# A gated delta net in stacked 32-row blocks, in a one-core decoder layer

## The chip, the cores and the metric

The kernel runs on one core of a Trainium2 chip. TensorE (PE) multiplies matrices, VectorE (DVE), ScalarE (ACT) and GpSimd (POOL) do the rest, and SyncE (SP) issues DMAs. The metric is the device time of one execution in microseconds: a median of 1965.41 over three runs (1960.49 to 1966.39).

## The reference, cut to what matters

One layer of a decoder for 1024 prompt tokens and 8 samples of 8 tokens: a norm, one input projection, three mixers (sparse attention, a gated delta net, S5), an output projection and an MLP. The delta net has 4 heads of 64. Queries and keys pass a short convolution and silu, then:

```python
q = l2norm(y[..., :DN_WIDTH].reshape(B, L, DN_HEADS, DN_DK)) * DN_DK ** -0.5
k = l2norm(y[..., DN_WIDTH:2 * DN_WIDTH].reshape(B, L, DN_HEADS, DN_DK))
# in chunks; gc is the running sum of the log decay, tri the lower triangle
decay = jnp.where(tri, jnp.exp(jnp.where(tri, diff, 0.0)), 0.0)     # diff = gc_i - gc_j
a_mat = jnp.where(strict, jnp.einsum('nbhid,nbhjd->nbhij', kb, kc) * decay, 0.0)
sol = lax.linalg.triangular_solve(a_mat + eye, rhs, left_side=True, lower=True)
u, w = sol[..., :dv], sol[..., dv:]
a_qk = jnp.where(tri, jnp.einsum('nbhid,nbhjd->nbhij', qc, kc) * decay, 0.0)
# chunk after chunk:
v_new = u_i - w_i @ S ;  o_i = (q_i * exp(g_i)) @ S + aqk_i @ v_new
S = S * exp(g_last) + (k_i * exp(g_last - g_i)).T @ v_new
```

## The kernel before, in words

Stages follow one another, each a block of five instruction streams with a barrier at its end: input norm with feature projection and S5, query projection, token projection, delta net, key preparation, attention of the samples, attention of the prompt, output projection and MLP. Arithmetic is f32; projections split f32 into two rounded parts and take three products.

The query projection (`query_projection`, L544, by `project`, L404) has 12 units (4 column chunks, 3 token groups). Beside its products DVE convolves six feature rows (L580) and ACT applies silu (L590). ACT and DVE copy the units out by turns.

The delta net (`delta_net`, L1093) takes chunks of 128 tokens, two by two in pairs: (0,1), (2,3), (4,5), (6,7), and the 64 sample rows alone. For a chunk PE turns features into rows (`rows_of`, L1500); ACT squares and copies them (`squares_of`, L1288), DVE sums squares per head and POOL takes the power -1/2 (L1237); DVE scales (`normalise`, L1377); POOL multiplies by gates (`scale`, L1233); PE turns everything back (`turn`, L1510), ACT copies (`features_of`, L1299). PE makes decay rows, with a second product adding a -1e30 table above the triangle (L1536, L1538), ACT their exponential (`decay_of`, L1310), PE the Gram products (`grams`, L1521), and DVE multiplies (`decayed`, L1394).

The inverse of the triangular matrix is built in seven levels over whole 128x128 matrices. In each, POOL masks A to the level's blocks, PE multiplies by T ("lower", L1565), ACT copies the result to U, PE joins (L1575, L1576), DVE subtracts from T and its transpose TT:

```python
pool.tensor_tensor(B[:n, x, :, :n], AT[:n, k % 4, :, :n], mask, ALU.mult).then_inc(b_ready, 1)
last = pe.matmul(m.ps[:n, 3 * x, h * P:h * P + n], B[:n, x, h, :n],
                 T[:n, x, h, :n] if s else m.ident[:n, :n], start=True, stop=True)
```

After a pair's levels comes its chain, chunk by chunk: w (L1584), v (L1626, L1629), state and output (L1633 to L1641), the state by DVE (L1434). The order is written out by hand: `after_level` puts the preparation of the next pair's chunks behind certain levels; the chain stands alone behind them. At the end DVE masks the sample rows' operands (L1468 to L1471), norms the outputs (`finish`, L1443) and PE turns them (L1651).

Of the kernel before, what the change touches and what calls it, by code (L numbers as in the profile page):

```python
# [22 lines left out]
P = 128  # L23
# [9 lines left out]
SEQ = 1024  # L33
# [33 lines left out]
def constant_tables():  # L67
# [42 lines left out]
    t["neg"] = np.where(p <= i, 0, NEG).astype(f)  # L110
    t["neg_s"] = np.where((p <= i) & (p // 8 == i // 8), 0, NEG).astype(f)
    t["level"] = np.concatenate([((i >> s) == (p >> s) + 1) & (i >> (s + 1) == p >> (s + 1))
                                 for s in range(LEVELS)], 1).astype(f)
    t["seq_col"] = np.concatenate([np.broadcast_to((np.arange(64)[None, :] // 8) == b, (P, 64))
                                   for b in range(8)], 1).astype(f)
    t["seq_row"] = np.concatenate([(p // 8) == b for b in range(8)], 1).astype(f)
    t["quarter"] = (p // 32 == np.arange(4)[None, :]).astype(f)
# [393 lines left out]
def token_projection(nc, m, tokens):  # L511
# [25 lines left out]
    def gpsimd(pool, _):  # L537
        pool.memset(m.small[64:128, TS, :], 0.0).then_inc(zeroed, 1)

# [4 lines left out]
def query_projection(nc, m):  # L544

    with ExitStack() as ctx:
        units = [(c, n) for c in range(4) for n in range(3)]
        convw = ctx.enter_context(nc.sbuf_tensor("convw", [P, 6, 4], F32))
        conv = m.mixT[:, 0:6, :]
        loaded, tap, conv_made, silu_made = (m.sem(f"conv_{n}") for n in ("loaded", "tap", "made", "silu"))  # L550
# [14 lines left out]
        def load(pool, _):  # L565
            pool.dma_start(convw[:], m.conv_w).then_inc(loaded, 16)

# [4 lines left out]

        def vector(dve, u):

            if u % 3 == 2 or u // 3 * 2 >= 6:
                return
            f = u // 3 * 2 + u % 3
            if f == 0:
                dve.wait_ge(loaded, 16)
            for j in range(4):  # L580
                src, w = m.dnx[:, f, j:j + CONVN], convw[:, f, j:j + 1]
                if j == 0:
                    dve.tensor_scalar(conv[:, f, :CONVN], src, w, None, ALU.mult).then_inc(tap, 1)
                else:
                    last = dve.scalar_tensor_tensor(conv[:, f, :CONVN], src, w, conv[:, f, :CONVN], ALU.mult, ALU.add)
                    last.then_inc(conv_made if j == 3 else tap, 1)
                if j < 3:
                    dve.wait_ge(tap, 3 * f + j + 1)
# [8 lines left out]
        def scalar(act, u):  # L597
            if u % 3 == 2 and u // 3 * 2 < 6:
                silu(act, u // 3 * 2)
                silu(act, u // 3 * 2 + 1)  # L600

        project(nc, m, "qp", m.w_in[:4], [P] * 4, units, evacuation, True,
                side={"gpsimd": load, "sync": load_next, "vector": vector, "scalar": scalar}, preload=m.query_raw)
# [489 lines left out]
def delta_net(nc, m):  # L1093
# [6 lines left out]
    with ExitStack() as ctx:  # L1100
# [3 lines left out]
        NT = TILES  # L1104
        flat_hT = m.mixT[:].rearrange("p k n -> p (k n)")
        conv, convs = m.mixT[:, 0:6, :], m.convs
        names = ["ones", "ones_s", "upto", "upto_s", "neg", "neg_s", "level", "seq_row"]
        C = {n: sb(n, [P, CONST_AT[n][1]]) for n in names}
        alog, dtb, normw = sb("alog", [P, H]), sb("dtb", [P, H]), sb("normw", [P, HD])
        minus_half = sb("minus_half", [P, NT * H])  # L1110
# [5 lines left out]
        qk = sb("qk", [P, 2, 512])  # L1116
        sq = sb("sq", [P, 512])
        ssq = sb("ssq", [P, 2, 8])
        rnorm = sb("rnorm", [P, 2, 8])

        kb, kbg, qg = sb("kb", [P, 256]), sb("kbg", [P, 4, 256]), sb("qg", [P, 256])
        kdec, vb = sb("kdec", [P, 4, 256]), sb("vb", [P, 4, 256])
        featT = sb("featT", [P, 6, P])
        qgT = sb("qgT", [P, 4, 2, P])
        decay = sb("decay", [P, H, P])
        AT, aqkT = sb("AT", [P, 4, H, P]), sb("aqkT", [P, 4, H, P])
        B, U, T, TT = (sb(n, [P, 2, H, P]) for n in ("B", "U", "T", "TT"))
        wT = sb("wT", [P, 2, 2, P])
# [8 lines left out]
        raw, qk_out, vb_out = sem("raw"), sem("qk_out"), sem("vb_out")  # L1137
        ssq_ready, rnorm_ready, normed = sem("ssq_ready"), sem("rnorm_ready"), sem("normed")
# [8 lines left out]
        masked, ss_ready = sem("masked"), sem("ss_ready")  # L1147
# [4 lines left out]
        wTm = B[:].rearrange("p a h n -> p (a h n)").rearrange("p (c b n) -> p c b n", c=2, b=NB)  # L1152
        qgm = U[:].rearrange("p a h n -> p (a h n)").rearrange("p (c b n) -> p c b n", c=2, b=NB)

        def kdecm(b):
            t = (AT if b < 4 else T)[:].rearrange("p a h n -> p (a h n)")
            return t[:64, (b % 4) * 256:(b % 4) * 256 + 256]

        def order(k, s):

            if k == TS:
                return TS * LEVELS + s + 1
            return (k // 2) * 2 * LEVELS + 2 * s + k % 2 + 1

        def order1(k, s):

            if k == TS:
                return TS * (LEVELS - 1) + s
            return (k // 2) * 2 * (LEVELS - 1) + 2 * (s - 1) + k % 2 + 1

        def pairs():
            return [(0, 1), (2, 3), (4, 5), (6, 7), (TS,)]

        def after_level(p, s, stages):

            if p + 1 < len(pairs()):
                a, b = (pairs()[p + 1] + (None,))[:2]
                if s in stages:
                    stages[s](a)
                if s - 4 in stages and b is not None:  # L1180
                    stages[s - 4](b)

        def second_of(p):

            return pairs()[p + 1][1] if p + 1 < len(pairs()) and len(pairs()[p + 1]) > 1 else None

        def levels(k):
            return SLEVELS if k == TS else LEVELS

        def heads(t):  # L1190
            return t.rearrange("p (h n) -> p h n", h=H)

        with nc.Block() as block:
# [33 lines left out]
            def _(pool):  # L1227
                link = Link(pool, vec_pool)
                link(pool.memset(o_all[64:128, TS, :], 0.0))
                link(pool.memset(minus_half[:], -0.5))  # L1230
                pool.memset(S[:], 0.0).then_inc(s_zero, 1)

                def scale(k):  # L1233
                    n, x, y = ROWS[k], k % 2, k % 4
                    bc = lambda c: gate[:n, c, k, :].unsqueeze(2).to_broadcast([n, H, HD])
                    pool.wait_ge(ssq_ready, k + 1)
                    pool.tensor_tensor(rnorm[:n, x, :], ssq[:n, x, :], minus_half[:n, :8], ALU.pow).then_inc(rnorm_ready, 1)  # L1237
# [4 lines left out]
                    kn = heads(qk[:n, x, 256:512])  # L1242
                    pool.tensor_tensor(heads(kb[:n, :]), kn, bc(BETA), ALU.mult).then_inc(scaled, 1)
                    pool.tensor_tensor(heads(qg[:n, :]), heads(qk[:n, x, 0:256]), bc(EGC), ALU.mult).then_inc(scaled, 1)
                    if k >= 4:
                        pool.wait_ge(wprod, k - 3)
                        pool.wait_ge(sprod, k - 3)
                    pool.tensor_tensor(heads(kdec[:n, y, :]), kn, bc(EDEC), ALU.mult).then_inc(scaled, 1)
                    pool.wait_ge(scaled, 4 * k + 1)
                    pool.tensor_tensor(heads(kbg[:n, y, :]), heads(kb[:n, :]), bc(EGC), ALU.mult).then_inc(scaled, 1)  # L1250

                scale(0)
                scale(1)
                for p, pair in enumerate(pairs()):
                    for s in range(levels(pair[0])):
                        for k in pair:
                            n, x = ROWS[k], k % 2
                            pool.wait_ge(a_ready, 4 * (k + 1))
                            if s:
                                pool.wait_ge(bt, order(k, s - 1))  # L1260
                            elif k >= 2:
                                pool.wait_ge(bt, order(k - 2, LEVELS - 1))
                            if s == 1:
                                pool.wait_ge(t_ready, order(k, 0))
                            mask = C["level"][:n, s * P:s * P + n].unsqueeze(1).to_broadcast([n, H, n])
                            pool.tensor_tensor(B[:n, x, :, :n], AT[:n, k % 4, :, :n], mask, ALU.mult).then_inc(b_ready, 1)  # L1266
                        after_level(p, s, {1: scale})
                for i, (t0, t1) in enumerate(((0, TS), (TS, NT))):
                    part = lambda c: gate[:, c, t0:t1].rearrange("p t h -> p (t h)")
                    pool.wait_ge(osq, i + 1)  # L1270
                    pool.tensor_tensor(part(T1), part(T0), minus_half[:, :H * (t1 - t0)], ALU.pow).then_inc(orn, 1)

            @block.scalar
            def _(act):
# [11 lines left out]
                act.activation(egl_s[:], m.ps[:, 0, 128:160].rearrange("p (b h) -> p b h", b=NB), ACT.Exp).then_inc(gexp, 1)  # L1286

                def squares_of(k):  # L1288
                    n, x = ROWS[k], k % 2
                    act.wait_ge(raw, k + 1)  # L1290
                    if k:
                        act.wait_ge(ssq_ready, k)
                    if k >= 2:
                        act.wait_ge(scaled, 4 * (k - 1))
                        act.wait_ge(turned, k - 1)
                    act.activation(sq[:n, :], m.ps[:n, 6, :], ACT.Square).then_inc(qk_out, 1)
                    act.activation(qk[:n, x, :], m.ps[:n, 6, :], ACT.Copy).then_inc(qk_out, 1)

                def features_of(k):  # L1299
                    n, y = ROWS[k], k % 4  # L1300
                    act.wait_ge(turned, k + 1)
                    if k:
                        act.wait_ge(gram, 2 * k)
                    if k >= 4:
                        act.wait_ge(oprod, k - 3)
                    act.activation(featT[:, 0:4, :n], heads(m.ps[:, 7, :])[:, :, :n], ACT.Copy).then_inc(feat_out, 1)
                    act.activation(featT[:, 4:6, :n], heads(m.ps[:, 6, :])[:, 0:2, :n], ACT.Copy).then_inc(feat_out, 1)
# [1484 lines left out]
```

## Time and profile before

| | |
|---|---|
| median of three runs | 1965.41 us |
| the profiled execution, on the device | 1963.47 us |
| its span in the trace | 1961.6 us |
| PE busy | 1768.7 us (90%) |
| DVE, ACT, POOL busy | 918.1, 537.9, 374.3 us |
| delta net, first gate instruction to last copy | 373 to 710.3 us |

A record is one instruction in the trace, with its start and its busy time; matmuls overlap, so the distance of their starts tells their cost, not the time of one. Idle time is put down to what ended it. The granted clock of PE has two levels, 2.4 GHz (1.00) and 1.2 GHz (0.50); a stretch shows the mean.

### The profile page before, as it was taken

How to read it: one execution, taken by the hardware profiler on the slowest of the kernel's cores; microseconds unless marked ns; L12 is line 12 of the kernel's file. 1: busy time of each engine (PE TensorE's matmuls, PEld its weight loads, DVE VectorE, ACT ScalarE, POOL GpSimd, SP SyncE). 2: the span in 40 equal slices, each digit the busy share in tenths (PEclk: the TensorE clock that was granted, in tenths of full speed). 3: DMA queues.
4: the chain of work that ended last, by engine and by line, in shares of the span. 5: the costliest groups of instructions: out<-in, count | busy, mean ns of one | idle time of the engine just before them, and what ended most of it. 6: DMA issues, size and time to landing. Idle time of an engine off the chain costs nothing. (4 is left out here: it accounts for less than half of the span.)

```text
span 1961.6 us, 29787 instructions
## 1 busy us (share of the span) xinstructions
PE 1768.7 (90%) x12570; PEld 1600.6 (82%) x12570; DVE 918.1 (47%) x1773; ACT 537.9 (27%) x1069; POOL 374.3 (19%) x343
## 2 busy tenths in 40 slices
PE   6999989469998766688998999999999999999998
PEld 5998989358888655556776999999999999999996
DVE  6950721034444433266775344444444444444447
ACT  5212321122222131166666033111111112211112
POOL 2010000043434110067774001000100010000000
PEclk7989999779999865589999999999999999999999
DMA  4000110320000020200002101111111111111102
GB/s 144 33 25 13 55 67 1 135 71 1 1 1 28 3 74 1 85 1 2 2 2 87 50 22 55 44 43 44 43 44 44 43 45 47 52 51 44 44 22 91
DMA packets 28592, 81.31 MB, mean 41 GB/s; under 512 B 6794, under 2 KB 15210, under 8 KB 23178
## 3 DMA queue, kind: packets, MB, share of 16 engines
q1 hardware_dynamic: 25954, 73.53, 11.2%
q10 hardware_dynamic: 1976, 4.92, 0.7%
q8 instruction: 99, 1.62, 0.3%
q0 software_dynamic: 528, 0.95, 0.2%
q14 instruction: 35, 0.29, 0.0%
HBM read 71.36 MB, written 10.12 MB: 42 GB/s over the span
## 5 line engine op out<-in xcount | busy, mean ns | idle before, releaser
L393 PE MATMUL ps<-mlp_mix_hi,mlp_w_hi 128*128 128x360 f32 (+1 forms) x768 | 252.5, 329 | 0.0
L395 PE MATMUL ps<-mlp_mix_hi,w_lo 128*128 128x360 f32 (+1 forms) x768 | 252.3, 328 | 0.0
L394 PE MATMUL ps<-mixT_lo,mlp_w_hi 128*128 128x360 f32 (+1 forms) x768 | 251.5, 327 | 0.0
L2439 DVE TENSOR_TENSOR x<-x,ps 128x512 f32<-128x512 f32 (+1 forms) x288 | 180.7, 655 | 138.7 <-PE ps L395 138.0
L2419 POOL TENSOR_TENSOR mlp_rect<-mlp_rect 128x360 f32<-128x360 f32 (+1 forms) x96 | 77.5, 807 | 774.8 <-ACT mlp_rect L2361 774.8
L393 PE MATMUL ps<-mlp_w_hi,mlp_hid_hi_lo 128*128 128x512 f32 x512 | 202.1, 395 | 0.0
L395 PE MATMUL ps<-mlp_w_hi,mlp_hid_lo 128*128 128x512 f32 x512 | 202.1, 395 | 0.0
L394 PE MATMUL ps<-w_lo,mlp_hid_hi_lo 128*128 128x512 f32 x512 | 202.1, 395 | 0.0
L2361 ACT ACTIVATE mlp_rect<-ps 128x360 f32<-128x360 f32 (+1 forms) x96 | 45.5, 474 | 556.1 <-PE ps L395 553.2
L2001 POOL TENSOR_SCALAR pa_probs<-pa_probs,pa_fac 128x640 f32<-128x640 f32 (+7 forms) x96 | 158.7, 1666 | 187.6 <-DVE pa_fac L1928 187.6
L2479 DVE TENSOR_TENSOR mlp_hid_lo<-mlp_rect,mlp_hid_hi_lo 128x368 fp32r<-128x368 f32 (+1 forms) x64 | 53.1, 830 | 234.8 <-ACT mlp_hid_hi_lo L2367 234.8
L393 PEld LDWEIGHTS ps<-mlp_mix_hi,mlp_w_hi 128*128 128x128 f32 x768 | 144.5, 188 | 0.8
L394 PEld LDWEIGHTS ps<-mixT_lo,mlp_w_hi 128*128 128x128 f32 x768 | 144.4, 188 | 0.7
L395 PEld LDWEIGHTS ps<-mlp_mix_hi,w_lo 128*128 128x128 f32 x768 | 144.1, 188 | 0.0
L395 PEld LDWEIGHTS ps<-mlp_w_hi,mlp_hid_lo 128*128 128x128 f32 x512 | 96.5, 188 | 22.5
L394 PEld LDWEIGHTS ps<-w_lo,mlp_hid_hi_lo 128*128 128x128 f32 x512 | 96.5, 188 | 22.5
L393 PEld LDWEIGHTS ps<-mlp_w_hi,mlp_hid_hi_lo 128*128 128x128 f32 x512 | 96.4, 188 | 22.4
L1266 POOL TENSOR_TENSOR dn_B<-dn_AT,dn_level 128x512 f32<-128x512 f32 (+1 forms) x59 | 73.5, 1261 | 129.2 <-DVE dn_aqkT L1401 48.5
L2013 ACT ACTIVATE pa_probs<-pa_probs,pa_nm 128x640 f32<-128x640 f32 (+7 forms) x128 | 92.4, 728 | 8.9 <-DVE pa_nm L1917 8.8
L2429 DVE TENSOR_TENSOR w_lo<-w_raw,mlp_w_hi 128x2048 fp32r<-128x2048 f32 x36 | 82.4, 2289 | 25.0 <-ACT mlp_w_hi L2336 25.0
L1860 PEld LDWEIGHTS ps<-ident,pa_probs 128*128 128x128 f32 x528 | 57.5, 142 | 37.4 <-issue 33.1
L393 PE MATMUL ps<-kvp_whi,h_hi 128*128 128x264 f32 x288 | 82.7, 287 | 5.8 <-DVE kvp_wlo L475 5.8
(467 smaller groups left out, 3738.2 us busy)
## 6 DMA issues: line engine op xcount, KB each, us to landing
w_raw<-in_w_up SPq DMA_DIRECT2D x16, 1024.0 KB, 4.8
w_raw<-in_w_down SPq DMA_DIRECT2D x16, 1024.0 KB, 4.7
feat_raw<-in_w_feat SPq DMA_DIRECT2D x12, 512.0 KB, 3.6
uT<-in_w_token SPq DMA_DIRECT2D x4, 1056.0 KB, 5.5
ck<-in_cache_nsa SPq DMA_DIRECT2D x16, 256.0 KB, 3.0
w_raw<-in_w_out SPq DMA_DIRECT2D x4, 1024.0 KB, 6.2
x<-in_x_prompt SPq DMA_DIRECT2D x4, 1024.0 KB, 7.5
out_y_p<-x SPq DMA_DIRECT2D x8, 512.0 KB, 2.6
```

Source lines behind the costliest of these rows:

```text
L393: pe.matmul(out, lhs[0], rhs[0], start=first, stop=False)
L394: pe.matmul(out, lhs[0], rhs[1], start=False, stop=False)
L395: return pe.matmul(out, lhs[1], rhs[0], start=False, stop=last)
L1266: pool.tensor_tensor(B[:n, x, :, :n], AT[:n, k % 4, :, :n], mask, ALU.mult).then_inc(b_ready, 1)
L1860: last = pe.transpose(m.ps[:, 4 + st % TURNS, (2 * s + g) * P:(2 * s + g + 1) * P], probs[:, slot(e, g), col:col + P], m.ident[:])
L2001: last = pool.tensor_scalar(probs[:, x, o:o + w], probs[:, x, o:o + w], fac[:, x, b:b + 1], None, ALU.mult)
L2013: act.activation(probs[:, x, o:o + w], probs[:, x, o:o + w], ACT.Exp, bias=nm[:, x, b, pieces(i)[j][1]:pieces(i)[j][1] + 1], scale=-1.0, a ...
L2361: act.activation(rect[:, (rank[u] - 1) % 2, :w], m.ps[:, bank_of(u), :w], ACT.Relu).then_inc(rectified, 1)
L2419: pool.tensor_tensor(part, part, part, ALU.mult).then_inc(rect_squared, 1)
L2429: dve.tensor_tensor(w_lo[:, s, :], w_raw[:, s, :], w_hi[:, s, :], ALU.subtract).then_inc(w_lo_made, 1)
L2439: dve.tensor_tensor(part, part, bank, ALU.add).then_inc(done, 1)
L2479: dve.tensor_tensor(hid_lo[:, g % 2, f, o:o + w], part, hi, ALU.subtract).then_inc(hidden_lo, 1)
```

## The change

In the delta net the first five levels work on 32x32 diagonal blocks, stacked by rows: the four blocks of a chunk lie on four groups of 32 partitions, heads and both chunks of a pair side by side in the columns. Two more steps join 32-row blocks to 64 and 64 to 128. One POOL instruction masks all five levels (`pack`). ACT's and DVE's steps take both chunks at once. Decay rows are one product per head, with no masking product: DVE bounds them by the diagonal value (`bound`), ACT takes the exponential, and POOL masks the query product afterwards (`causal`). The chain of a pair moves into the steps of the next pair. The sums of squares of queries and keys are made beside the query projection: ACT squares, PE sums by a two-head table and turns, DVE scales, and POOL takes the power -1/2 in the token projection. The output norm is done for tiles 0 to 5, 6 to 7 and the samples instead of 0 to 7 and the samples.

```diff
 # token projection
+        pool.wait_ge(m.qk_sums_made, 4)
+        pool.tensor_tensor(flat, flat, m.minus_half[:], ALU.pow)
 # query projection
+        def tensor(pe, u):
+            if u == 8:
+                pe.wait_ge(norm_table, 16)
+                pe.wait_ge(squared, 8)
+                ...
+                for g, (o, w) in enumerate(GROUPS_N):
+                    for f in range(4):
+                        last = pe.matmul(m.ps[32 * f:32 * f + 32, 4 + g, :w], two_heads[:], squares[:, f, o:o + w], start=True, stop=True)
+            if u == 10:
+                pe.wait_ge(sums_kept, 3)
+                for t in range(TILES):
+                    last = pe.transpose(m.ps[:ROWS[t], 4 + t // 4, ...], sums[:, t * P:t * P + ROWS[t]], m.ident[:])
 # ACT, scalar(act, u)
+            if u in (6, 7):
+                for f in (2 * (u - 6), 2 * (u - 6) + 1):
+                    act.activation(squares[:, f, :SEQ], conv[:, f, :SEQ], ACT.Square).then_inc(squared, 1)
+                    act.activation(squares[:, f, SEQ:], m.convs[:, f], ACT.Square).then_inc(squared, 1)
 # delta net, POOL
-                            pool.tensor_tensor(B[:n, x, :, :n], AT[:n, k % 4, :, :n], mask, ALU.mult).then_inc(b_ready, 1)
+                def causal(k):
+                    pool.tensor_tensor(part, part, C["upto" if k < TS else "upto_s"]..., ALU.mult).then_inc(causal_made, 1)
+                def pack(k):
+                    pool.tensor_tensor(B[:n, :lv, i], ATc[:n, i].unsqueeze(1).to_broadcast([n, lv, H, 32]),
+                                       mask.unsqueeze(2).to_broadcast([n, lv, H, 32]), ALU.mult).then_inc(b_ready, 1)
 # DVE
-                    link(dve.tensor_reduce(ssq[:n, x, :], sq[:n, :].rearrange("p (h d) -> p h d", h=8), AX.X, ALU.add))
+                def bound(pair):
+                    for k in pair:
+                        last = dve.tensor_tensor(decay_at(k)[:n, :, :n], heads(m.ps[:n, G0 + k % 2, :])[:, :, :n], gate[GC]..., ALU.min)
+                            dve.tensor_tensor(T[:n], T[:n], bank[:n], ALU.subtract).then_inc(t_ready, 1)
+                for p in range(len(PAIRS)):
+                    (a, b), (c, d) = following(p), chained(p)
+                    at_step(p, 0, level, [(normalise, a)])
+                    at_step(p, 1, level, [])
+                    if a is not None:
+                        bound((a, b))
+                    at_step(p, 2, level, [(next_state, c), (take_o, c), (normalise, b)])
+                    at_step(p, 3, level, [(decayed, a)])
+                    at_step(p, 4, level, [])
+                    if STEPS[p] > SMALL_LEVELS:
+                        spread_blocks(p)
+                    at_step(p, 5, level, [(decayed, b), (next_state, d), (take_o, d)])
+                    at_step(p, 6, level, [])
+        FINISH = ((0, 6), (6, TS), (TS, NT))
 # PE
-                        last = pe.matmul(row, m.ident[:n, :n], C["neg" if k < TS else "neg_s"][:n, :n], start=False, stop=True)
+                def lower(p, s):            # step s < 5; joined(p, s) likewise, with T and U32
+                    for i, k in enumerate(PAIRS[p]):
+                        for h in range(H):
+                            for q in range(ROWS[k] // 32):
+                                rows = slice(32 * q, 32 * q + 32)
+                                last = pe.matmul(m.ps[rows, L0, at:at + 32], B[rows, s, i, h, :],
+                                                 T[rows, 0, i, h, :] if s else m.ident[rows, rows], start=True, stop=True)
+                    for s, (first, then) in enumerate((([(w_products, c)], [(rows_of, a)]),
+                                                       ([(v_products, c)], [(turn, a)]),
+                                                       ([(s_products, c)], [(rows_of, b), (grams, a)]),
+                                                       ([(w_products, d)], [(turn, b)]),
+                                                       ([(v_products, d)], [(grams, b)]),
+                                                       ([(s_products, d)], []), ([], []))):
+                        at_step(p, s, lower, first)
+                        at_step(p, s, joined, then)
+                        if s == 0:
+                            decay_rows((a, b))
```

## Rows read from the trace of the kernel before

**Rows 1.** The top of the page.
```profile
span 1961.6 us, 29787 instructions
```
**Rows 2.** Timeline of PE in the delta net: start us, busy us, line, operation.
```profile
426.88 1.16 PE L1565 MATMUL ps<-ident,dn_B 128*128 128x128 f32 x8
...
431.17 1.06 PE L1565 MATMUL ps<-dn_T,dn_B 128*128 128x128 f32 x8
...
476.96 1.16 PE L1584 MATMUL ps<-dn_TT,dn_kbg 128*128 128x128 f32 x8
...
483.63 1.16 PE L1584 MATMUL ps<-dn_TT,dn_kbg 128*128 128x128 f32 x8
...
489.13 2.32 PE L1565 MATMUL ps<-ident,dn_B 128*128 128x128 f32 x16
...
654.73 0.83 PE L1584 MATMUL ps<-dn_TT,dn_kbg 128*128 128x128 f32 x6
```
**Rows 3.** Busy time of each engine and granted clock by stretch, whole kernel.
```profile
core 0: us, PE busy (x) PEld busy (x) DVE busy (x) ACT busy (x) POOL busy (x), PEclk, DMA share, GB/s
...
105.00:113.00 8.00, 8.00 (x159) 8.00 (x156) 7.91 (x15) 0.00 (x0) 0.00 (x0) 0.50 0.01 3
385.00:427.00 42.00, 21.37 (x103) 18.98 (x104) 9.11 (x30) 10.56 (x28) 9.19 (x11) 0.60 0.36 111
427.00:490.00 63.00, 55.94 (x460) 52.71 (x460) 29.49 (x56) 15.98 (x36) 27.00 (x25) 1.00 0.00 1
...
666.00:678.00 12.00, 7.36 (x50) 6.34 (x48) 2.39 (x6) 0.83 (x3) 1.44 (x2) 0.57 0.04 7
```
**Rows 4.** Waits of PE from 427 to 666 us: total, times, longest.
```profile
PE ps L1565 <- POOL dn_B L1266: 13.2, 12, 1.5
```
**Rows 5.** Narrow matmuls in S5: PE's timeline, then one line's records by the us.
```profile
95.65 0.33 PE L1037 MATMUL ps<-s_cw,s_bb 128*32 128x32 f32 x16
95.80 0.94 PE L1037 MATMUL ps<-mixT_raw,s_bb 128*32 128x224 f32 x16
...
102.00:103.00 1.00, 1.00 (x44) 1.00 (x42) 1.00 0.00 0
...
107.00:108.00 1.00, 1.00 (x24) 1.00 (x25) 0.50 0.00 0
```
**Rows 6.** Groups by line and form, 360 to 712 us: busy us, mean ns.
```profile
L1423 DVE TENSOR_TENSOR dn_TT<-dn_TT,ps 128x512 f32<-128x512 f32 x48 | 33.0, 687 | 18.9 <-PE ps L1576 17.6
L1434 DVE SCALAR_TENSOR_TENSOR dn_S<-dn_S,dn_gate,ps 64x64 f32<-64x64 f32 x32 | 9.0, 280 | 31.6 <-PE ps L1637 31.3
...
L1346 ACT ACTIVATE dn_vnew<-ps 128x256 f32<-128x256 f32 x8 | 3.1, 384 | 13.6 <-PE ps L1629 13.6
...
L1266 POOL TENSOR_TENSOR dn_B<-dn_AT,dn_level 128x512 f32<-128x512 f32 x56 | 71.3, 1290 | 109.0 <-DVE dn_aqkT L1401 48.5 <-PE ps L1565 40.6 <-DVE dn_T L1416 19.1
...
L1271 POOL TENSOR_TENSOR dn_gate<-dn_gate,dn_minus_half 128x32 f32<-128x32 f32 x1 | 7.4, 7404 | 17.8 <-DVE dn_gate L1455 17.8
```
**Rows 7.** Timeline of ACT and DVE at the query projection's end.
```profile
232.84 0.96 ACT L560 ACTIVATE qT<-ps 64x368 f32<-64x368 f32 x2
...
248.50 1.07 DVE L562 TENSOR_SCALAR qT<-ps 64x360 f32<-64x360 f32 x2 [2.18 <-PE ps L395]
```
**Rows 8.** Timeline of PE in the delta net's prologue, first chunk.
```profile
392.82 1.54 PE L1507 MATMUL ps<-ident,mixT_raw 128*128 128x128 f32 x6 [1.56 <-ACT dn_egl_s L1286]
...
403.64 0.80 PE L1536 MATMUL ps<-dn_upto,dn_gate 128*128 128x128 f32 x2 [1.24 <-ACT dn_qgT L1308]
...
407.35 0.79 PE L1526 MATMUL ps<-dn_featT 64*128 64x128 f32 x2
```
**Rows 9.** Timeline of DVE and PE at the delta net's end.
```profile
683.04 2.28 DVE L1453 TENSOR_TENSOR mixT_raw<-dn_o 128x2048 f32<-128x2048 f32 x1
...
697.77 2.29 DVE L1460 TENSOR_TENSOR dn_o<-dn_o,tokens 128x2048 f32<-128x2048 f32 x1
...
696.96 0.68 PE L1615 MATMUL ps<-dn_vnew,dn_aqkT 64*64 64x64 f32 x8
```

More of the change, by code:

```diff
@@ L1165, in order1 @@
[L1165 to L1188, printed above, removed]
+            return AT[:64].rearrange("p a h n -> p (a h n)")[:, b * 256:b * 256 + 256]
+        PAIRS = [(0, 1), (2, 3), (4, 5), (6, 7), (TS,)]
+        STEPS = [7, 7, 7, 7, SLEVELS]
+        def step_no(p, s):
+            return sum(STEPS[:p]) + s + 1
+        def tail_no(p, s):
+            return sum(STEPS[:p]) - p + s
@@ L1190, in heads, with following, chained, at_step @@
+        def following(p):
+            return (PAIRS[p + 1] + (None,))[:2] if p + 1 < len(PAIRS) else (None, None)
+        def chained(p):
+            return PAIRS[p - 1] if p else (None, None)
+        def at_step(p, s, level, pieces):
+            if s < STEPS[p]:
+                level(p, s)
+            for piece, k in pieces:
+                if k is not None:
+                    piece(k)
         def heads(t):
             return t.rearrange("p (h n) -> p h n", h=H)
+        FINISH = ((0, 6), (6, TS), (TS, NT))
@@ new lines, in keep_diagonal @@
+                def keep_diagonal(p):
+                    c = len(PAIRS[p])
+                    act.wait_ge(t_ready, step_no(p, min(SMALL_LEVELS, STEPS[p]) - 1))
+                    act.wait_ge(zeros, 3)
+                    if p >= 2:
+                        act.wait_ge(vprod, 2 * (p - 1))
+                    for q in range(2):
+                        rows = slice(32 * q, 32 * q + 32)
+                        last = act.activation(TT[rows, p % 2, :c, :, rows], T[rows, 1, :c], ACT.Copy)
+                    last.then_inc(diag, 1)
@@ L1517, in turn @@
                                              kb[:n, 0:128], kb[:n, 128:256], qg[:n, 0:128], qg[:n, 128:256])):
[L1518 removed]
+                        last = pe.transpose(m.ps[:, R1 - c // 4, (c % 4) * P:(c % 4) * P + n], src, m.ident[:n, :n])
                     last.then_inc(turned, 1)
[L1521 to L1528 removed]
@@ L1530, in even_grams, with decay_rows @@
-                def even_grams(k):
+                def decay_rows(pair):
+                    for k in pair:
+                        if k is None:
+                            continue
+                        n = ROWS[k]
+                        if k:
+                            pe.wait_ge(a_ready, 2 * (k // 2) * 2)
+                        for h in range(H):
+                            last = pe.matmul(m.ps[:n, G0 + k % 2, h * P:h * P + n], gate[:n, GC, k, h:h + 1].to_broadcast([n, n]),
+                                             m.ident[:n, :n], start=True, stop=True)
+                        last.then_inc(drow, 1)
@@ new lines, in _ @@
+                for b in range(NB):
+                    for c in range(2):
+                        last = pe.matmul(vbank[:, c * P:(c + 1) * P], wTm[:, c, b, :], Ss[:, b, c, :],
+                                         start=False, stop=b == NB - 1, skip_group_check=True)
+                last.then_inc(vprod, 1)
+                pe.wait_ge(o_out, TS)
+                for b in range(NB):
+                    for c in range(2):
+                        pe.matmul(obank[:, c * P:(c + 1) * P], qgm[:, c, b, :], Ss[:, b, c, :],
+                                  start=b + c == 0, stop=False, skip_group_check=True)
@@ new lines, in _ @@
+                pe.wait_ge(v_ready, NT)
+                pe.wait_ge(v_ready, TS)
+                pe.wait_ge(o_out, TS)
+                pe.wait_ge(s_ready, TS)
+                for b in range(NB):
+                    for c in range(2):
+                        last = pe.matmul(m.ps[:, 4 + b // 2, (b % 2) * 256 + c * P:(b % 2) * 256 + (c + 1) * P],
+                                         kdecm(b)[:, c * P:(c + 1) * P], vnew[:n, c * P:(c + 1) * P],
+                                         start=True, stop=True)
@@ L1658, in key_prep @@
+                last.then_inc(sprod, 1)
+                pe.wait_ge(causal_made, NT)
+                for h in range(H):
+                    last = pe.matmul(obank[:, h * HD:(h + 1) * HD], aqkT[:n, k % DEEP, h, :n], vnew[:n, h * HD:(h + 1) * HD],
+                                     start=False, stop=h == 3, skip_group_check=True)
+                last.then_inc(oprod, 1)
+                for t in range(FINISH[0][1], NT):
+                    turn_rows(t)
 def key_prep(nc, m, held):
```

690 lines of the change are left out of this document (388 added, 302 removed).

## The prediction, as put on record

> **What bounds the kernel now.** I read the page's top line first, then the timeline, the busy time by stretch, the waits and the groups by form. The profiled execution spans 1961.6 us [rows 1]; it took 1963.47 us on the device, 1.9 us around the span, and the median of the three runs, 1965.41, lies 1.9 above it. I sum against 1963.5.
>
> The change lives in one stage, the delta net. Its triangular solves start at 426.88 and those of the second pair of chunks at 489.13, so a pair takes 62.2 us; the levels of the fourth pair end at 654.73 [rows 2]. Nothing of another stage runs beside it, so what it loses comes off the end of the kernel. In the pairs TensorE (PE) is the bound: busy 55.9 of the first pair's 63 us at clock 1.00 [rows 3]. Of what it waits for, the POOL masks are the largest part, 13.2 us in all pairs [rows 4].
>
> **The pairs, part by part.** A level before is 8 whole-array products for "lower" and 16 for the join; each f32 product is two records, and eight records stretch over 1.06 us with 0.275 for one, so they start 0.112 apart [rows 2]. Seven lowers and six joins (the last one halved) are 7x16 + 5x32 + 16 = 288 records, 32 us. After, five levels run in 32x32 blocks, a lower of 64 records of 32 columns and a join of 128; the two joining steps have 32 and 48, then 16 and 16. 5x64 + 4x128 + 32 + 48 + 32 = 944 records: more of them, and what one costs decides the change.
>
> Prices of a narrow record. Sixteen with 32 weight columns and 32 moving ones start between 95.65 and 95.80, 9.4 ns each: a short burst. In a long row-tiled stream with 8 moving columns they come 44 to the us (22.7 ns), and at the low clock 24 (42 ns) [rows 5]. Nothing in the trace has four 32x32 tiles on different rows and columns. The bounds are therefore 9.4 ns, the four side by side, and 56 ns, one after the other at the low clock (32 columns of a 128-column record's 112 ns, doubled). I take 15 ns, between burst and stream and nearer the burst, whose weights are as narrow as ours: 14.2 us a pair.
>
> PE's other work in a pair: 28 transposes x 0.112 = 3.1; decay rows 16 x 0.112 = 1.8, half of before, since the product with the -1e30 table goes; Grams 32 x 0.112 = 3.6; the chain of two chunks. One chunk's chain runs from 476.96 to the next one's start at 483.63 [rows 2], and about 4.5 of the 6.7 us are PE's own, the rest Grams and its wait on ACT's copy: 9.0. Sum 31.7 at the full clock, 17.5 of it wide. Before, the two chains stood alone behind the levels; now their pieces lie between lower and join of the next pair's steps, where PE would wait for ACT: their waits vanish, their PE time stays.
>
> What PE still waits for. Both chunks of a pair go together: lower, ACT copy of 256 columns (0.38), join, DVE subtraction of 512 (0.69) [rows 6]. Where a transpose, Gram or chain piece lies behind the join the 0.69 is covered. In steps 5 and 6 nothing is, and DVE has the second chunk's decay product (two of 0.69, four 32-row copies) and the state update (4 x 0.28) queued ahead of the last subtraction; in step 2 ACT's copies of the turned features stand ahead of vnew and U. I count 6 us a pair. POOL loses 14 masks of 1.29 and the pow and gains two packed masks (640 columns, 1.6) and two causal ones (1.29) [rows 6]; with 3.7 of scalings it has 9.5 us a pair, so its 13.2 us of holding PE up go. DVE has about 20, ACT 10. PE is late next.
>
> The clock. Whole-array work, PE busy 89%, ran at 1.00; the prologue, 51% busy, at 0.60; the sample rows' solve, 61% busy in 64-wide products, at 0.57; 8-column records, PE busy throughout, at 0.50 [rows 3]. So narrow work doesn't hold the high level. After, a pair has 17.5 us of wide records in some 40, and sparse ends: I expect the clock to fall and rise within each pair, 0.75 in the mean. PE then needs 31.7/0.75 = 42 us, and this covers half of the waits: 45. The first pair has no chain inside: 33. Pairs 33 + 3x45 = 168 against 654.7 - 426.9 = 227.8: **-60**. Bounds: full clock and 9.4 ns, 8.9 + 17.5 + 6 = 32 us a pair (the first 28, its waits uncovered: 124, -104); low clock and 56 ns, 92 a pair (+121, below).
>
> **Query projection.** ACT's eight squares (four of 1024 columns, four of 64, some 4.5 us) queue behind its copy at 232.84 and end at 238.3. PE ends unit 8 at about 236.5, waits for them 1.8 us, and units 9 to 11 and the stage's end are queued behind. The 24 sum records of 360 columns, by sixteen of 224 over 0.94 us with 0.35 for one [rows 5], cost 63 ns each: 1.5 us (7 if they don't overlap). Nine transposes 1.0; DVE's four small scalings behind its last copy (248.50) [rows 7] 0.8. Together **+5**, bounds +3 to +11. The pow of 72 columns, by 7.40 us for 32 [rows 6], takes 17 us on POOL, covered by the token projection, as is the small table's load by the units before; uncovered the pow would cost these 17.
>
> **Prologue and tail.** The rows of the first chunk start at 392.82, the first level 34.1 us later; two chunks go one after the other, 17 us each. In each the decay rows take 3.7 (403.64 to 407.35) [rows 8] and squares, sums and pow some 3.5; without them 9.9, twice 19.8. All decay rows at once, halved, 3.4; copies into blocks 1.1, packed mask 1.6, handoffs 1.6: 27.5, **-6.5**. At the end the sample rows' levels, 12 us alone, go into the steps of pair 3's chain. But DVE norms six tiles ahead of the masks and two behind, where before all eight (683.04 to 700.06) lay beside PE's sample products (to 697.6) [rows 9]: those products need some 14 us behind the masks, of which two tiles' norms cover 5, so DVE waits 9. Nearly level: **-1**, bounds -10 to +8.
>
> Sum: +5 - 60 - 6.5 - 1 = -62, so **1901 us**.
>
> Two pages of the Trainium skill speak against this. "TensorE: Matmul & The Clock Gate" says in "Wait — 56ns, not 53.3ns?" that matmul starts never come closer than about 25 ns however small they are; the burst at 9.4 ns differs, the stream at 22.7 nearly agrees [rows 5]. By it 944 records are an estimated 23.6 us a pair.
> "TensorEngine Tiling (Array Packing)" says in "Restrictions and Gotchas" that different row tiles can't use one PSUM bank at once. The new blocks put four row tiles into one bank; the trace's row-tiled stream writes four banks, so no row here shows it.
>
> **Rivals.**
> *A floor on narrow records.* Each starts 22.7 ns after the last, as the stream's do: 21.4 us a pair. For it: the stream is long, the burst short; against: the stream loads 128 weight columns, the blocks 32. At the full clock 21.4 + 17.5 + 6 = 45, the forecast's own time; at the low clock 21.4 + 35 + 4 = 60, pairs 42 + 3x60 = 222, -6, in all -8: **1955**. The first page's rule is this one.
> *Full clock throughout, records as in the burst:* -104 for the pairs, -106 in all, **1857**. For it: a pair at 1.00 before; against: narrow columns didn't hold the clock.
> *Slower: the four tiles go one after another.* If row groups can't write one bank together, and the clock falls, a record costs 56 ns: 944 x 56 = 53 us, with 35 wide and 4 of waits 92 a pair; 73 + 3x92 = 349, +121, in all **2082**; at the stream's 42 ns 2034. It turns the sign from about 25 ns a record at the low clock, where a pair is 62 us again. Its rule is the second page's. For it: no row shows the opposite; against: each tile has its own columns, hence its own PSUM partitions.
> *The handoffs bind:* seven serial steps keep a pair at 62 us whatever the matmuls cost, so no change, **1963**. Against: PE was busy 89% of a pair, so handoffs weren't what filled it.
>
> **How the numbers follow.** Forecast 0.46 (own range 1875 to 1930), full clock 0.17, floor at the low clock 0.17, serial tiles 0.14, handoffs 0.06. 1855 to 1960 takes in the first two and most of the third. Some 6 us (0.3%) can be told from no change. Faster 0.46 + 0.17 + 0.14 = 0.77; same 0.07; slower 0.16.
>
> **What would show it.** Records of the new lower and join lines: 67 to the us by the forecast, 44 by the floor, 18 if serial at the low clock. From one pair's first lower to the next 45 us, clock 0.75, no wait of PE on POOL, short ones on DVE in the last two steps. The first lower 27.5 us behind the first rows; the query projection 5 us longer with a stall on ACT's squares; DVE waiting 9 us for the sample products. Narrow records above 25 ns at the low clock, or a clock of 0.50 in all pairs, would make it wrong.

## The result and the profile after

The changed kernel takes 1898.24 us (median of four runs, 1888.5 to 1903.34) against 1965.9 for the kernel before: ratio 0.9654, 95% interval 0.9611 to 0.9698. The profiled run took 1897.29; its span is 66.2 us shorter [rows 1]. The page's top, and its queue of PE's instructions (packets, MB, share):
```profile
span 1895.4 us, 34835 instructions
...
q8 instruction: 119, 1.95, 0.4%
```
PE's timeline of the changed kernel gives the terms. L1687 is the first decay row, L1721 "lower" with the identity (a pair's start), L1766 the last pair's w, L1743 and L1746 the two halves of a join, L1675 a turn.
```profile
397.12 3.78 PE L1687 MATMUL ps<-ident,dn_gate 128*128 128x128 f32 x16 [1.56 <-ACT dn_egl_s L1348]
...
420.62 1.07 PE L1721 MATMUL ps<-ident,dn_B 32*32 32x32 f32 x64 [3.82 <-POOL dn_B L1320]
...
427.52 0.26 PE L1743 MATMUL ps<-dn_U,dn_T 32*32 32x32 f32 x8 [0.48 <-ACT dn_U L1384]
...
428.56 0.24 PE L1746 MATMUL ps<-dn_T,dn_U 32*32 32x32 f32 x6
428.78 0.63 PE L1675 MATMUL ps<-ident,dn_qk 128*128 128x128 f32 x4
...
458.14 1.07 PE L1721 MATMUL ps<-ident,dn_B 32*32 32x32 f32 x64
...
551.83 0.33 PE L1743 MATMUL ps<-dn_U,dn_T 32*32 32x32 f32 x8
551.96 0.31 PE L1746 MATMUL ps<-dn_T,dn_U 32*32 32x32 f32 x8
552.07 0.31 PE L1743 MATMUL ps<-dn_U,dn_T 32*32 32x32 f32 x8
...
580.26 1.12 PE L1766 MATMUL ps<-dn_TT,dn_kbg 128*64 128x128 f32 x8 [0.21 <-DVE dn_TT L1561]
```
In the kernel before, PE's timeline has the last pair's w and the sample rows' w here ([rows 2] begin inside the first of them, at its third record, so the pairs took 227.5 us and not 227.8):
```profile
654.41 1.15 PE L1584 MATMUL ps<-dn_TT,dn_kbg 128*128 128x128 f32 x8
...
675.92 1.97 PE L1584 MATMUL ps<-dn_TT,dn_kbg 64*128 64x64 f32 x8 [0.51 <-DVE dn_TT L1423]
```
The delta net's first work behind the gates comes 4.3 us later than before (392.82 [rows 8]), the first lower 23.5 us behind that (34.1 before), the last pair's w 159.6 us behind the first lower (227.5 before). A join's 128 records start within 1.1 us, 8.6 ns apart, at the full clock; at the low clock eight take 0.107 us, 13.3 ns each.

| term | forecast | measured |
|---|---|---|
| query projection | +5 | +4.3 |
| prologue | -6.5 | -10.6 |
| pairs | -60 | -67.9 |
| behind the last pair's solve | -1 | +8.0 |
| sum | -62 | -66.2 |

The first term is read at the delta net's start, and that moves: in the nine profiled runs with the same code up to there it lies between 397.1 and 402.1 us, the changed kernel's being the earliest. The query projection by itself, from its first product to the token projection's first, takes 61.5 us (196.3 to 257.8) for 56.3 (198.0 to 254.3), so +5.2.

Stretches from one pair's first lower to the next (the last ends with the sample rows' first lower), to set beside [rows 3]:
```profile
core 0: us, PE busy (x) PEld busy (x) DVE busy (x) ACT busy (x) POOL busy (x), PEclk, DMA share, GB/s
420.62:458.14 37.52, 29.25 (x1021) 26.20 (x1021) 15.07 (x33) 8.22 (x23) 10.30 (x11) 0.68 0.01 3
458.14:497.58 39.44, 33.12 (x1094) 29.95 (x1093) 17.73 (x44) 9.54 (x27) 8.98 (x11) 0.85 0.02 4
497.58:535.94 38.36, 32.68 (x1093) 29.53 (x1092) 17.73 (x44) 9.65 (x27) 9.88 (x11) 0.86 0.02 4
535.94:579.42 43.48, 35.57 (x1056) 32.07 (x1055) 12.34 (x32) 6.92 (x20) 4.21 (x6) 0.58 0.10 34
```
And PE's waits from 420 to 580 us (total, times, longest), where [rows 4] had 13.2 us on POOL:
```profile
PE ps L1728 <- DVE dn_TT L1558: 5.6, 4, 1.4
PE ps L1746 <- issue: 4.7, 3, 3.1
PE ps L1743 <- issue: 4.3, 3, 2.1
PE ps L1721 <- POOL dn_B L1320: 3.8, 1, 3.8
PE ps L1721 <- issue: 3.0, 4, 1.1
```
POOL's one wait is that of the prologue. New at this size is "issue", idle time without a releaser: 14.4 us in twelve stretches, all inside or right behind narrow streams. PE's instructions (weight loads, matmuls and semaphore instructions), counted to each of the twelve, are 6594, 6850, 7361, 9154 and so on: each time 193 or 194 over a multiple of 256. PE's 30,649 instructions over q8's 119 packets are 257.6 a packet, and each of the twelve ends 1.2 to 1.5 us after one of these packets has landed. So the rows suggested waits for the next packet of instructions, and three experiments below test it.

DVE's timeline at the end (L1609 begins the norms, L1625 the masks, L1635 the state updates), beside [rows 9]:
```profile
601.24 1.76 DVE L1609 TENSOR_TENSOR mixT_raw<-dn_o 128x1536 f32<-128x1536 f32 x1
...
614.26 0.68 DVE L1625 TENSOR_TENSOR dn_B<-dn_wT,mixT_raw 128x512 f32<-128x512 f32 x1
...
632.88 0.68 DVE L1635 TENSOR_TENSOR mixT_raw<-mixT_raw,dn_egl_s 64x512 f32<-64x512 f32 x1 [8.90 <-PE ps L1854]
```
The 8.90 us wait for the sample products is there as forecast (9); the masks come late, behind 13 us of norms.

### The profile page after: what moved, and what is told of

It is laid out like the page before. It is cut to its first block and busy times, and to the rows that moved or that the text cites. A ratio compares the mean times of both kernels' runs of the same rounds, so it can differ in the third digit from the quotient of the medians.

```text
span 1895.4 us, 34835 instructions
## 1 busy us (share of the span) xinstructions
PE 1690.9 (89%) x15219; PEld 1521.4 (80%) x15219; DVE 876.1 (46%) x1742; ACT 517.3 (27%) x1043; POOL 322.0 (17%) x291
## 5 line engine op out<-in xcount | busy, mean ns | idle before, releaser
L2071 PEld LDWEIGHTS ps<-ident,pa_probs 128*128 128x128 f32 x528 | 57.4, 142 | 37.5 <-issue 33.1
L2071 PE MATMUL ps<-ident,pa_probs 128*128 128x128 f32 x528 | 70.4, 280 | 18.7 <-issue 15.7
```

The lines of the kernel that those rows point to most:

```text
L2071: last = pe.transpose(m.ps[:, 4 + st % TURNS, (2 * s + g) * P:(2 * s + g + 1) * P], probs[:, slot(e, g), col:col + P], m.ident[:])
```

## Experiments

All times are to be held against 1898 for the changed kernel and 1965 for the one before. Edits are to the changed kernel.

**tile_by_tile.** Lower and join run through one row tile, then the next:
```
- for i, k in pair: for h in heads: for q in row_tiles: matmul(rows q ...)
+ for q in row_tiles: for i, k in pair: for h in heads: matmul(rows q ...)
```


> Same products of the five 32-wide levels in another order: all of one row tile, then all of the next, where the changed kernel goes round the four tiles from one product to the next. Theory (9.0 ns a record because four tiles, each with its own rows and columns, run side by side; products of one tile follow each other): a record by itself takes a quarter of the 112 ns of 128 columns, 28 ns at the full clock; 832 records of a pair cost 16 us more, joined takes 3.6 us and not 1.15: about 1950 to 1960. Rival (the order doesn't matter, records start 9 ns apart whichever tile they use): joined stays at 1.15 us at the full clock, the time within 4 us of 1897.


2008.0 us, ratio 1.021 (1.019 to 1.023): the same products in another order cost 110 us and make the change a loss. PE's timeline (two lowers, at the full and at the low clock), then the first two pairs' stretches:
```profile
431.04 1.91 PE L1721 MATMUL ps<-dn_T,dn_B 32*32 32x32 f32 x64
...
464.80 3.06 PE L1721 MATMUL ps<-dn_T,dn_B 32*32 32x32 f32 x64
```
```profile
424.20:485.70 61.50, 56.68 (x1021) 53.71 (x1022) 15.15 (x33) 8.22 (x23) 10.29 (x11) 0.56 0.01 2
485.70:558.50 72.80, 70.73 (x1093) 66.80 (x1092) 17.80 (x44) 9.64 (x27) 9.45 (x11) 0.55 0.01 2
```
A record now takes 27 ns at the full clock ((1.91 - 0.2)/63, 0.2 being one record's own length), as expected, and 45 to 53 at the low one. The time missed the expected 1950 to 1960, which had counted the 27 ns at the full clock alone: some 61 us of the loss. The rest goes with the clock, 0.55 with PE busy 97% of the second pair, against 0.85 at 84%. Side by side, then, the tiles are worth a factor of three to four, and PE has no wait on "issue" at all in these pairs.

**three_times.** Round each product of the 32-wide levels:
```
+ for again in range(3):
```


> Issues each product of the five 32-wide levels three times over with the same result: 1664 more records in a pair of chunks, 3328 more PE instructions beside 2192. Theory A (a record costs what it takes to run, 9.0 ns at the full clock and 13.3 at the low one, and the idle times without a releaser are a side cost): 15 to 22 us more in a pair, 55 to 62 us from first lower to first lower, and idle times without a releaser of some 35 us in all pairs: about 1975 to 2000. Theory B (in a long run PE is held to the pace at which its instructions arrive, packets of 256 no closer than 3.3 to 3.6 us, so 13 to 14 ns an instruction and 26 to 28 ns a record of two): 5520 instructions are 21.6 packets, 71 to 78 us a pair, idle times without a releaser above 60 us in all: 2025 to 2050. Rival C (handoffs between the engines bind, narrow records are hidden in them): under 5 us a pair, below 1917.


2122.3 us, above both theories, and inconclusive: with the repetitions on the same tile records came 24 ns apart at the low clock, not 13.3, and waits without a releaser were only 16.5 us in all four pairs. The edit had mixed two effects.

**three_rounds.** The repetition goes round the tiles:
```
- for q in range(ROWS[k] // 32):
+ for q in 3 * list(range(ROWS[k] // 32)):
```


> Again three times each product of the five 32-wide levels, but going round the four row tiles between a product and its repetition (before, the repetition came at once and on the same tile, 24 ns a record at the low clock, so that run couldn't tell running from supply). A pair has 2496 narrow records in these levels and 5520 PE instructions. Theory A (9.0 ns a record at the full clock, 13.3 at the low one, whatever the length of the stream): 15 to 22 us more a pair, 55 to 62 us from first lower to first lower, about 1970 to 1990. Theory B (instructions come in packets of 256, no closer than 3.3 to 3.6 us in any run so far): 21.6 packets a pair, 71 to 78 us, idle times of PE without a releaser above 10 us in each pair, about 2025 to 2055.


2098.4 us. Stretches of the first two pairs; PE's three longest waits without a releaser from 420 to 785 us; the DMA queue in the second pair:
```profile
421.14:505.94 84.80, 53.75 (x2685) 49.04 (x2685) 15.16 (x33) 8.22 (x23) 10.29 (x11) 0.62 0.02 4
505.94:597.78 91.84, 63.07 (x2757) 57.69 (x2757) 17.81 (x44) 9.65 (x27) 9.50 (x11) 0.65 0.02 4
```
```profile
PE ps L1743 <- issue: 36.7, 22, 2.5
PE ps L1746 <- issue: 36.4, 19, 2.7
PE ps L1721 <- issue: 21.7, 14, 2.6
```
```profile
q8 instruction: 22, 0.36, 1.5%
```
Beyond the range of either theory, with the sign of theory B: PE is idle a third of the pair and its idle time without a releaser is 101 us in 59 stretches, all at 193 or 194 over a multiple of 256. It isn't idle time alone: of the 52 us that the second pair takes more than in the changed kernel, 30 are busy time of PE. Its packets come 91.84/22 = 4.2 us apart in this pair and never closer than 3.3. At that least spacing 128 records of two instructions are 26 ns each. The section "Instruction fetch mechanics" of the Trainium skill's page "Runtime: NRT & Kernel Launch" has instructions refilled in blocks of 256, as counted here, and calls the cost mostly hidden; in this stream it isn't.

**state_late.** The 1 MB load of the sample states moves on SP's queue (and with it the 256 KB load of a mask table):
```
- sp.wait_ge(raw, NT)
+ sp.wait_ge(s_ready, TS)
  sp.dma_start(Ss, m.state_dn).then_inc(s_in, 16)
```


> Moves the 1 MB load of the sample states from the middle of the last pair's steps to behind the last state update. Theory (PE's 12 idle times of 0.45 to 3.08 us inside the narrow streams, without a releaser, are waits for its next instructions, which come in packets of 16 KB; the longest, 3.08 us from 543.5 on, is a packet held up behind this load): that wait falls to 1.5 us or less, the others stay, the last pair takes 41 to 42.5 us in place of 43.9, the whole 1.5 to 2.5 us less: about 1895. Rival 1 (idle times of PE for another reason, not the load): a wait of about 3 us stays at that place, no change. Rival 2 (the load is then late for the sample products): PE waits for it at the end, 1897 or more.


1892.0 us (1888.6 to 1899.5), ratio 0.9624 (0.9605 to 0.9643), which overlaps the changed kernel's interval: the whole can't tell them apart. The place says more. The changed kernel's 3.08 us wait from 543.5 on lies where these loads move (540.1 to 545.8), and ends 1.5 us after a packet that came at the loads' end, from 544.2 to 545.2; in this run that place has none, and the last pair takes 41.8 us (539.63 to 581.47) for 43.5. PE's waits in it without a releaser:
```profile
PE ps L1720 <- issue: 1.2, 1, 1.2
...
PE ps L1745 <- issue: 0.6, 1, 0.6
```
In the changed kernel they are 4.2 us there. Each of these waits moves a little from run to run. With the load in its old place, masks_first has a wait of 2.76 us there, but levels_last and norms_in_chunk have none. That the load caused the wait is not shown.

**chain_behind.** The chain of w, v, state and output products stands behind its own pair's last step on PE, ACT and DVE; on PE:
```
- at_step(p, s, lower, [(w_products, c)]) ...
+ for k in PAIRS[p]: w_products(k); v_products(k); s_products(k)   # behind step 6
```


> Takes the chain of a pair (w, v, state and output products) out of the next pair's steps and puts it behind the pair's own last step, as before the change; blocks, masks and norms stay as changed. Theory (the chain's pieces cover handoffs, and its own waits are covered): PE waits 2.2 us more in each chunk's chain, and about 0.5 us more at some six handoffs of a pair: 7 to 8 us a pair, 28 to 32 us in all, 1925 to 1930. Rival (the handoffs are covered by the turns and Grams alone, and instruction packets arrive while PE waits in the chain): idle times without a releaser shrink by what the chain's waits add, 1895 to 1905.


1924.6 us (ratio 0.9798, 0.9753 to 0.9843): the theory's number. A pair takes 47 to 50 us. The second pair's stretch, the last pair's w, and PE's waits in the pairs that are new or longer:
```profile
474.05:522.16 48.11, 37.89 (x1093) 33.86 (x1092) 17.74 (x45) 9.77 (x27) 9.50 (x10) 0.72 0.01 3
```
```profile
606.71 1.12 PE L1775 MATMUL ps<-dn_TT,dn_kbg 128*64 128x128 f32 x8 [0.77 <-DVE dn_TT L1567]
```
```profile
PE ps L1752 <- ACT dn_U L1387: 8.1, 16, 0.8
...
PE ps L1785 <- ACT dn_wT L1374: 3.8, 8, 0.5
```
Of the 26 us, 5 lie ahead of the first lower (425.65 for 420.62), in code that both share. From there to the last pair's w (606.71) it is 181.1 us for 159.6. So some 21 of the pairs' 68 us come from putting the chain between lower and join, and the rest from the blocks, the masks and the single decay product together, which no run takes apart. The theory counted waits alone: of the 8.7 us that the second pair takes more, 3.9 are idle time of PE, and 4.8 are its busy time, at a clock of 0.72 for 0.85.

**norms_in_chunk.** Squares, sums and power go back to the chunk; the query projection loses its sums and turns.
```
+ link(dve.tensor_copy(qk[:n], m.ps[:n, R0, :]))
+ link(dve.tensor_tensor(qk[:n], qk[:n], qk[:n], ALU.mult))
+ link(dve.tensor_reduce(ssq, ...))
...
+ pool.tensor_tensor(ssq, ssq, m.minus_half[:n, :8], ALU.pow).then_inc(npow, 1)
```


> Undoes one part of the change: the norms of queries and keys are made in each chunk again (DVE copies, squares and sums the turned rows, POOL takes the power, DVE waits for it), and the query projection has no squares, sums or turns. Theory: the query projection is 4 to 5 us shorter, the prologue 9 us longer (per chunk three DVE operations of 0.69, two of 0.17, 1.7 for the power and the handoffs, 4.5 in all), and in the pairs DVE's subtractions wait behind the power twice a pair, of which the wide pieces behind the join cover most: 0 to 4 us a pair. In all 1905 to 1915. Rival 1 (norms in the chunk are hidden, the part only cost its 5 us): prologue at most 4 us longer, 1890 to 1898. Rival 2 (DVE's waits lie on the path of every level): over 6 us a pair, 1920 and more.


1909.4 us (0.971, 0.9669 to 0.975), as expected. Gates start 3.7 us earlier (the query projection itself takes 56.9 us for 61.5), the first lower comes 32.8 us behind the first decay row (393.46) and not 23.5, the pairs take 4 us more. PE in the prologue:
```profile
404.49 1.08 PE L1671 MATMUL ps<-ident,dn_qk 128*128 128x128 f32 x4 [6.14 <-POOL dn_qg L1286]
...
426.22 1.01 PE L1717 MATMUL ps<-ident,dn_B 32*32 32x32 f32 x58 [3.82 <-POOL dn_B L1309]
```
The wait for a chunk's rows is 6.1 us, 1.8 in the changed kernel: the part pays. Its interval overlaps the changed kernel's (0.9611 to 0.9698), so these rows show it, not the whole.

**levels_last.** In the last round the chains run first, then the sample rows' levels:
```
+ for k in (6, 7): w_products(k); v_products(k); s_products(k)   # ahead of lower(4, 0)
```


> Undoes one piece of the tail: the last pair's two chains run by themselves again, as before the change, and the sample rows' three levels behind them; the rest as changed, the six tiles' norms still ahead of the masks. In the changed kernel the two chains with the levels inside take 20.6 us, where before the change chains took 11.0 and levels, to the masks, 13.1. Theory (inside each other they mostly add up, because a chain piece and a level piece wait for DVE in turn and PE runs at the low clock): chains 11 to 14 us, levels 9 to 12 us, in all 20 to 25, and the whole within 4 us of the changed kernel's 1898. Rival (the levels are hidden in the chains as forecast): the chains alone take 19 us or more and the levels 12 behind them, so 10 us longer, about 1908.


1897.8 us (0.966, 0.9632 to 0.9689), no change. PE's timeline: chain, levels, and the sample rows' w:
```profile
583.33 1.12 PE L1775 MATMUL ps<-dn_TT,dn_kbg 128*64 128x128 f32 x8 [0.77 <-DVE dn_TT L1567]
...
595.50 0.44 PE L1730 MATMUL ps<-ident,dn_B 32*32 32x32 f32 x16
...
602.15 0.69 PE L1775 MATMUL ps<-dn_TT,dn_kbg 64*64 64x64 f32 x8 [1.30 <-DVE dn_T L1559]
```
Chains 12.2 and levels 6.7 are 18.8 us one after the other; inside each other they took 20.6 (580.26 to 600.90). Nothing was gained there. The clock wasn't the same, though (the chains here, then the nested stretch of the changed kernel):
```profile
582.00:595.00 13.00, 10.74 (x75) 9.61 (x73) 2.45 (x7) 1.53 (x4) 0.00 (x0) 0.72 0.01 1
```
```profile
580.00:601.00 21.00, 17.83 (x173) 16.23 (x173) 4.34 (x16) 2.69 (x8) 0.00 (x0) 0.52 0.00 1
```
What the nesting would give at an equal clock, no run shows.

**masks_first.** On DVE (on PE and ACT the tiles' turns and copies go behind the sample products likewise):
```
- finish(0, *FINISH[0])
  (masks)
+ finish(0, *FINISH[0])
  finish(1, *FINISH[1])
```


> Moves, of the changed kernel, DVE's masks for the sample rows ahead of its norms of the prompt tiles, and PE's turning of those tiles behind the sample products (ACT's copies likewise). Theory (the tail grew because 13 us of norms stand ahead of the masks): masks start at about 602 us of the span and not at 614.3, PE ends its sample products near 621 and not at 633.4, DVE's wait of 8.9 us for them is gone, the last turn comes near 634 and not at 642.4; 1897 falls by 8 to about 1889. Rival (DVE's work is the same in any order, and the tiles' turns and copies, now at the end, are late instead): the last turn stays at 640 or later and the time within 2 us of 1897.


1888.7 us (0.9601, 0.958 to 0.9623); the interval touches the changed kernel's, the rows decide. DVE's wait for the sample products is gone, and from the sample rows' w to the last turn it is 33.2 us (598.26 to 631.47) for 41.5 (600.90 to 642.39): the expected 8. PE:
```profile
603.96 1.11 PE L1832 MATMUL ps<-dn_vb,dn_TT 64*64 64x64 f32 x8 [5.00 <-DVE dn_AT L1625]
...
631.47 0.47 PE L1821 MATMUL ps<-ident,dn_o 64*128 64x64 f32 x2 [8.71 <-DVE dn_o L1614]
```
**tail_spread.** On top of it, the first four tiles' norms go between the sample rows' levels and two of the three masks into the last chain (besides, the 1 MB state load goes behind the seventh state update):
```
- FINISH = ((0, 6), (6, TS), (TS, NT))
+ FINISH = ((0, 4), (4, TS), (TS, NT))
+ finish_squares(0)   # behind level(4, 0)
+ finish_scale(0)     # behind level(4, 1)
+ mask_k(); mask_q()  # ahead of next_state(7)
```


> A version on top of masks_first: norms of the first four prompt tiles go into DVE's gaps between the sample rows' levels, the key and query masks into its gaps in the last chain, so that one mask (1.4 us) stands between the sample rows' w and PE's sample products; the state load starts behind the seventh state update. Theory (the tail is DVE's work behind the last chain): PE's wait for the masks falls from 5.0 to about 1.5 us, and DVE, with four tiles less to norm, begins the state updates when PE's sample products end, so the last turn is 5 to 7 us earlier; with the load out of the last pair 1.5 us more: 1888.7 falls to about 1881. Rival (the norms now delay the sample rows' levels or the last state update by as much): the chain of the last chunk ends 4 us later or more, 1886 to 1890.


1883.5 us (0.9577, 0.9542 to 0.9611), the fastest version run. The same stretch is 24.9 us:
```profile
603.07 0.45 PE L1792 MATMUL ps<-dn_TT,dn_kbg 64*64 64x64 f32 x8 [0.38 <-DVE dn_S L1521]
605.21 1.08 PE L1860 MATMUL ps<-dn_vb,dn_TT 64*64 64x64 f32 x8 [1.69 <-DVE dn_B L1654]
...
627.93 0.47 PE L1849 MATMUL ps<-ident,dn_o 64*128 64x64 f32 x2 [5.37 <-DVE dn_o L1604]
```
Its interval overlaps that of masks_first, so the further gain is shown by the rows, not by the whole.

## Why the prediction was right, term by term

The forecast of 1901 is 3 us off because errors of both signs cancelled: 8 and 4 us too little gain in pairs and prologue, 9 too much at the end. That the total is so close is luck; where the gain comes from, and that narrow records are cheap side by side, was right.

*The narrow record* was taken as 15 ns and is 8.6. With 17.5 us of wide work, 944 x 8.6 ns gives 25.6 us at the full clock; over the measured 0.85 that is 30 of the 33 us that PE is busy in the second pair. The rival of four serial tiles falls: four 32x32 tiles in one PSUM bank do run together, and tile_by_tile shows what it would have been, 61 to 73 us a pair (not 92; and its 2034 for 42 ns a record should read 2029 by its own sum, 53 us less than 2082). The rule of the Trainium skill behind it ("TensorEngine Tiling (Array Packing)", "Restrictions and Gotchas") doesn't fit these rows. The floor of 22.7 ns falls as a floor on starts, with 8.6, but comes back as a mean: when narrow records run on for long, as in three_rounds, 26 ns is the least that the packets leave. The 25 ns of the Trainium skill's page "TensorE: Matmul & The Clock Gate" ("Wait — 56ns, not 53.3ns?"), given there for the starts themselves, don't fit these rows either.

*The clock* was forecast as 0.75 in the mean, falling and rising within each pair; the four stretches are 0.68, 0.85, 0.86 and 0.58, 0.74 by their lengths. Right in the mean; the second and third pairs kept more of it, the last less.

*The waits:* none on POOL in the pairs, short ones on DVE and ACT in steps 5 and 6, as said. Of the 6.3 us that PE is idle in the second pair, 3.4 are "issue", a wait the prediction didn't know; the other 2.9 are what it counted. The first pair took 37.5, not 33: without a chain its ACT copies are uncovered (four waits of 0.5) and it has 3.3 us of "issue". The last took 43.5, with the low clock and the long wait for a packet.

*The prologue:* 10.6 us saved and not 6.5. Squares, sums and power were taken as 3.5 us a chunk; a chunk without them takes 7.6 and 8.5 us, not 9.9. norms_in_chunk puts 4.6 a chunk on them as it makes them.

*The query projection:* PE's stall on the squares was forecast as 1.8 us and the sums as 1.5, the turns as 1.0. They are 1.7, 2.0 and 1.1:
```profile
236.31 2.04 PE L610 MATMUL ps<-dnx,two_heads 128*32 128x368 f32 x24 [1.71 <-issue]
```
ACT's last square ends at 236.21 us, so this "issue" is a wait with a releaser that the view didn't find: the word alone proves no packet. The power took 11.9 us on POOL, not 17, and is covered.

*The tail* is the step that failed. "At the end the sample rows' levels, 12 us alone, go into the steps of pair 3's chain" was booked as a gain of all 12. Stretches of the kernel before, first the chains, then the levels; and DVE's first state update:
```profile
654.41:665.44 11.03, 9.24 (x75) 8.41 (x73) 2.94 (x9) 2.28 (x6) 0.00 (x0) 1.00 0.01 1
665.44:675.92 10.48, 5.95 (x49) 5.09 (x48) 2.90 (x8) 0.75 (x2) 1.44 (x2) 0.60 0.03 6
```
```profile
699.98 0.68 DVE L1478 TENSOR_TENSOR mixT_raw<-mixT_raw,dn_egl_s 64x512 f32<-64x512 f32 x1
```
Chains and levels took 21.5 us and take 20.6: the gain is 0.9. The rows of before could have said so: PE was busy 9.2 of the chains' 11.0 us and 6.0 of the levels' 10.5, so at these prices laying one inside the other could save 6.3 at most. On top of this the chains ran at a clock of 1.00 before, and at 0.52 with the levels inside; how much is the clock's, the runs don't tell.

The other half of the term was right: "DVE waits 9" is 8.9. From the sample rows' w to DVE's first state update it is 32.0 us (600.90 to 632.88) for 24.1 (675.92 to 699.98): this wait, plus 1.3 for norms in two parts, less 2.3 for which DVE no longer waits for w. The norms' 13 us ahead of the masks aren't a further cost, as DVE has them to do in either order; they cost what they no longer cover behind the masks, and masks_first gives back 8.3. So -0.87 and +7.92, and +0.90 behind the delta net in code that didn't change, make 7.95. (The prediction's own -12 and +9 make -3, not -1.) Its bounds of -10 to +8 just hold the 8.0.

## What to carry to other kernels

Small matmuls were cheap here only where neighbours in the stream lay on different row and column tiles: order the loops so that the tile changes from one product to the next. Count instructions as a resource of their own: PE's streams that needed 256 of them in less than some 3.3 to 4 us ran dry here, and idle time without a releaser that recurs at a fixed remainder of the instruction count is the sign of it. Before booking one stretch as hidden inside another, look at how much idle time the other has. When work moves ahead in an engine's queue, charge the wait that it then no longer covers, and not its length as well, since the engine owes that in either order.

## What was not expected of the hardware

- Instruction packets of 256 never came closer than 3.2 us to each other in any run, 25 ns for a record of two instructions, while 128 records that had arrived ran in 1.1 us. Why the spacing is that, the runs don't tell.
- The longest such wait of the changed kernel (3.08 us) lay on a 1 MB load, and was gone with the load elsewhere; but in two other runs that load brought none, so its part stays open.
- In tile_by_tile PE was busier (97% against 84%) and the granted clock lower (0.55 against 0.85) than in the changed kernel for the same products.
